# Three edits of a two-block transformer kernel: fewer columns in the last layer's products, expert counts ahead of ranks, down products first in the expert loop

## What is computed

```python
# first block: each token goes to its two best experts of 32 (in one of 4 groups)
y = (jax.nn.silu(hf @ wg) * (hf @ wu)) @ wd        # wg, wu: 1024x256, wd: 256x1024
acc + gate_col[:, None] * y
# second block: 16 meta tokens are put ahead of the 512, and cut off at the end
h = jnp.concatenate([meta, x], axis=1)
for each of two layers:
    h = h + rms_norm(mixer(rms_norm(h, pre), *mix), post)
    h = h + rms_norm(conv_ffn(rms_norm(h, f_pre), w_up, c_w, c_b, w_down), f_post)
return h[:, N_META:]
```

## Time and profile before

| | |
|---|---|
| median of 3 runs | 3109.65 us (3108.88 to 3119.19) |
| the profiled execution, its own time | 3110.36 us |
| its span in the trace | 3108.5 us |
| PE busy | 2854.5 us (92%) |
| DVE, ACT, POOL busy | 1035.6, 620.8, 268.8 us |
| expert loop, first gate-up matmul to last down product read | 619.28 to 940.04 us |
| last layer, out2 to the last product | 2473.4 to 3095.3 us |

### The profile page before, as it was taken

The page is one execution under the profiler, slowest core; times in us unless marked ns, Lnnn a source line. Parts: engine busy times, 40 slices in busy tenths (PEclk is TensorE's granted clock), DMA queues, the critical chain, the costliest instruction groups (busy, mean ns, idle before and its releaser), DMA issues.

```text
span 3108.5 us, 37906 instructions
## 1 busy us (share of the span) xinstructions
PE 2854.5 (92%) x14859; PEld 2136.6 (69%) x14859; DVE 1035.6 (33%) x2148; ACT 620.8 (20%) x1304; POOL 268.8 (9%) x368
## 2 busy tenths in 40 slices
PE   4999887678994999999999999999989899999998
PEld 2554683423332886687888788888877687888787
DVE  6355642311114342604333201113437604333202
ACT  1121220101112453602111001111127402111000
POOL 3121220011220000000000000000006400000000
PEclk7999998689997998999999999999978899999999
DMA  5133102478963111011212122122210011212122
GB/s 226 69 123 122 55 1 122 160 293 356 377 246 126 68 67 56 2 68 55 79 70 73 62 108 108 60 76 68 81 41 2 1 68 58 78 67 81 54 109 81
DMA packets 49449, 312.15 MB, mean 100 GB/s; under 512 B 12192, under 2 KB 14496, under 8 KB 18336
## 3 DMA queue, kind: packets, MB, share of 16 engines
q1 hardware_dynamic: 39520, 290.28, 24.5%
q0 software_dynamic: 9216, 17.85, 1.5%
q10 hardware_dynamic: 576, 2.10, 0.2%
HBM read 351.08 MB, written 16.78 MB: 118 GB/s over the span
## 4 chain that ended last, share of the span: by engine, by line
PE 65%; DVE 2%; ACT 1%; issue 0%; DVEq 0%; POOL 0%; POOLq 0%; ACTq 0%
PE ps L489 35%; PE ps L1001 18%; PE ps L1044 2%; PE ps L966 1%; PE ps L1168 1%; PE ps L984 1%; PE ps L952 1%; PE ps L1140 1%; PE ps L1163 1%; PE ps L991 1%; PE ps L1176 0%; PE ps L1195 0%; PE ps L897 0%; PE ps L1166 0%; PE ps L1118 0%
## 5 line engine op out<-in xcount | busy, mean ns | idle before, releaser
L489 PE MATMUL ps<-u,ring 128*128 128x264 f32 (+1 forms) x5248 | 1253.6, 401 | 27.4 <-DVE u L1675 20.7
L489 PEld LDWEIGHTS ps<-u,ring 128*128 128x128 f32 x5248 | 998.9, 191 | 272.5 <-issue 97.5
L1001 PE MATMUL ps<-work,ring 128*128 128x264 f32 x2432 | 557.6, 389 | 10.8 <-DVE work L1678 8.9
L1001 PEld LDWEIGHTS ps<-work,ring 128*128 128x128 f32 x2432 | 466.4, 192 | 93.5 <-DVE work L1678 9.7
L1675 DVE TENSOR_SCALAR work<-tmp,par 128x528 f32<-128x528 f32 (+2 forms) x136 | 74.9, 551 | 663.6 <-ACT tmp L1578 335.7
L1681 DVE SCALAR_TENSOR_TENSOR work<-tmp,par,work 128x528 f32<-128x528 f32 (+2 forms) x320 | 245.5, 767 | 50.0 <-issue 46.4
L829 PE MATMUL ps<-work,u 128*64 128x512 f32 x640 | 175.4, 615 | 32.3 <-DMA work<-in_experts,rs 30.1
L2285 DVE RECIPROCAL rs<-rs 128x264 f32<-128x264 f32 x8 | 14.4, 1803 | 529.7 <-ACT rs L1520 529.0
L1678 DVE TENSOR_TENSOR work<-work 128x128 f32<-128x128 f32 (+7 forms) x366 | 141.6, 425 | 62.2 <-ACT work L1450 18.4
L1578 ACT ACTIVATE tmp<-ps 128x528 f32<-128x528 f32 x80 | 48.9, 612 | 499.6 <-PE ps L489 499.6
L829 PEld LDWEIGHTS ps<-work,u 128*64 128x64 f32 x640 | 56.7, 142 | 109.5 <-issue 106.6
(11 more groups left out here) (355 smaller groups left out, 2811.5 us busy)
## 6 DMA issues: line engine op xcount, KB each, us to landing
ring<-in_stream SPq DMA_DIRECT2D x169, 1024.0 KB, 4.8
work<-in_experts SPq DMA_DIRECT2D x25, 2048.0 KB, 14.5
work<-in_experts SPq DMA_DIRECT2D x25, 1024.0 KB, 9.3
ring<-in_experts SPq DMA_DIRECT2D x7, 2048.0 KB, 12.6
ring<-in_experts SPq DMA_DIRECT2D x7, 1024.0 KB, 8.7
work<-rows_out SPq DMA_DIRECT2D x4, 1024.0 KB, 8.0
h<-in_x_fm SPq DMA_DIRECT2D x1, 2048.0 KB, 10.7
rows_in<-work ACTq DMA_DIRECT2D x4, 512.0 KB, 2.6
```

The source lines that it names most:

```text
L489: m = pe.matmul(pair(q, half, cnt), ring[:, (n + b // 16) % WSLOTS, b % 16 * P:(b % 16 + 1) * P], x[:, lo:lo + cnt], start=(k == 0), stop= ...
L1001: return pe.matmul(pair(q0 + t, half, HALF), block(t, kk), rhs[kk][:, half * HALF:(half + 1) * HALF], start=(kk == 0), stop=(kk == parts - 1))
```

## The change

Three edits. (1) `product_halves`, `head_tiles` and `out_tile` take a `skip`: the first half of a tile leaves out its first 14 columns (out2, up2) or 16 (down2). (2) PE does the four count matmuls ahead of the ten of the ranks, with a signal of its own; DVE works on counts while PE does ranks, computes the packs by a rounding (three operations on 128x32) in place of seven comparisons, does the softmax of the choices later, and the overflow numbers after `move`; `moves_ready` 1 is now `move` and 2 is `over_id`. (3) In the expert loop, the gate-up product of step s+1 comes after the down product of step s, on ACT and DVE alike; POOL has one wait more ahead of the last `gather_expert`, and waits for `moves_ready` 2 only behind the first row gathers.

```diff
-                    parts = [(0, 0, ncols // 2), (1, ncols // 2, ncols // 2)]
+                    parts = [(0, skip, ncols // 2 - skip), (1, ncols // 2, ncols // 2)]
...
+            for j in range(CHUNKS):
+                m = pe.matmul(ps[:, 7, 128:160], ones, r32[5][:, j, :], start=(j == 0), stop=(j == CHUNKS - 1))
+            m.then_inc(sem("places_done"), 1)
...
             for s in range(len(MSTEPS)):
-                if s + 1 < len(MSTEPS):
-                    gate_up(s + 1)
                 hidden_turned(s)
                 if s + 2 < len(MSTEPS):
                     rows_turned(s + 2)
                 down(s)
+                if s + 1 < len(MSTEPS):
+                    gate_up(s + 1)
...
+                skip = {8: META - CONV_F + 1, 10: META}.get(n, 0)
...
+                skip = META - CONV_F + 1 if n == 10 else 0
...
             for s in range(len(MSTEPS)):
+                if s + 2 < len(MSTEPS):
+                    rows_out_of_psum(s + 2)
                 if s + 1 < len(MSTEPS):
                     gate_silu(s + 1)
-                if s + 2 < len(MSTEPS):
-                    rows_out_of_psum(s + 2)
...
-            ts(e32[1], e32[0], float(MROWS), None, ALU.is_gt)
-            for v in range(2, SEQ // MROWS):
-                dve.drain()
-                stt(e32[1], e32[0], float(MROWS * v), e32[1], ALU.is_gt, add)
+            ts(e32[1], e32[0], -0.5 - MROWS / 2, 1.0 / MROWS, add, mul)
+            dve.drain()
+            ts(e32[1], e32[1], ROUND, None, add)
+            dve.drain()
+            ts(e32[1], e32[1], -ROUND, 0.0, add, hi_)
...
                 hidden_out_of_psum(s)
+                rows_ready(s)
                 if s + 1 < len(MSTEPS):
                     hidden(s + 1)
-                rows_ready(s)
...
             pool.wait_ge(sem("moves_ready"), 1)
-            pool.wait_ge(sem("moves_ready"), 2)
...
+            pool.wait_ge(sem("moves_ready"), 2)
...
                     pool.wait_ge(sem("dn_done"), s + 1)
+                    if MSTEPS[s + 1]:
+                        pool.wait_ge(sem("over_loaded0"), 16 * MSTEPS[:s + 2].count(1))
+                        pool.wait_ge(sem("over_loaded1"), 16 * MSTEPS[:s + 2].count(1))
```

More of the change, by code:

```diff
@@ L473, in unit_wait, with out_tile @@
                 pe.wait_ge(sem(f"unit_loaded{n % WSLOTS}"), 16 * (n // WSLOTS + 1))
-            def out_tile(q, n, b0, rhs, ncols, free, normed=None):
+            def out_tile(q, n, b0, rhs, ncols, free, normed=None, skip=0):
                 pe.wait_ge(sem("tile_read"), free)
@@ L488, in out_tile @@
                             pe.wait_ge(sem("normed"), normed + k + 1)
-                        m = pe.matmul(pair(q, half, cnt), ring[:, (n + b // 16) % WSLOTS, b % 16 * P:(b % 16 + 1) * P],
+                        at0 = 0 if half else skip
+                        m = pe.matmul(ps[:, 2 * (q % 2) + half, at0:at0 + cnt], ring[:, (n + b // 16) % WSLOTS, b % 16 * P:(b % 16 + 1) * P],
                                       x[:, lo:lo + cnt], start=(k == 0), stop=(k == len(rhs) - 1))
@@ L791, in _ @@
             pe.wait_ge(sem("slots_ready"), 1)
+            for j in range(CHUNKS):
+                m = pe.matmul(ps[:, 7, 128:160], ones, r32[5][:, j, :], start=(j == 0), stop=(j == CHUNKS - 1))
+            m.then_inc(sem("places_done"), 1)
             for c in range(CHUNKS):
                 for j in range(c + 1):
[L794 to L797, removed]
+                    m = pe.matmul(ps[:, 1, 32 * c:32 * c + 32], ones if j < c else ccol("strict", 0, P), r32[5][:, j, :],
+                                  start=(j == 0), stop=(j == c))
             m.then_inc(sem("places_done"), 1)
@@ L998, in product_halves @@
                 q0, i0 = Q0[stage], EDGE_SQ(n)
+                skip = {8: META - CONV_F + 1, 10: META}.get(n, 0)
                 def mm(t, half, kk):
-                    return pe.matmul(pair(q0 + t, half, HALF), block(t, kk), rhs[kk][:, half * HALF:(half + 1) * HALF],
-                                     start=(kk == 0), stop=(kk == parts - 1))
+                    lo = 0 if half else skip
+                    return pe.matmul(ps[:, 2 * ((q0 + t) % 2) + half, lo:HALF], block(t, kk),
+                                     rhs[kk][:, half * HALF + lo:(half + 1) * HALF], start=(kk == 0), stop=(kk == parts - 1))
                 for t in range(FULL):
@@ L1035, in product_halves, with head_tiles @@
                 half_sums(i1 + 1, 1, False, True)
-            def head_tiles(stage, n, normed):
+            def head_tiles(stage, n, normed, skip=0):
                 q0, n0, i0 = Q0[stage], U0[stage], EDGE_SQ(n) + 2 + 2 * DT
@@ L1042, in mm @@
                     b = 8 * (t % 2) + kk
-                    out = pair(q0 + t, half, HALF) if t < 2 else ps[:, 4 + half, 0:HALF]
-                    return pe.matmul(out, ring[:, (n0 + t // 2) % WSLOTS, b * P:(b + 1) * P],
-                                     u[:, kk, half * HALF:(half + 1) * HALF], start=(kk == 0), stop=(kk == DT - 1))
+                    bank, lo = (2 * ((q0 + t) % 2) if t < 2 else 4) + half, 0 if half else skip
+                    return pe.matmul(ps[:, bank, lo:HALF], ring[:, (n0 + t // 2) % WSLOTS, b * P:(b + 1) * P],
+                                     u[:, kk, half * HALF + lo:(half + 1) * HALF], start=(kk == 0), stop=(kk == DT - 1))
                 for t in range(3):
@@ L2147, in _ @@
             dve.drain().then_inc(sem("slots_ready"), 1)
-            dve.wait_ge(sem("places_done"), 2)
+            dve.wait_ge(sem("choice_exp"), 1)
+            dve.tensor_reduce(r1[4], r4[1], AX, add)
+            dve.wait_ge(sem("choice_exp"), 2)
+            ts(r1[5], r1[6], 1.0, None, add)
+            dve.drain()
+            tt(r1[4], r1[4], r1[5], mul)
+            dve.drain()
+            dve.reciprocal(r1[7], r1[4])
+            dve.drain()
+            tt(r1[8], r1[7], r1[6], mul)
+            dve.wait_ge(sem("places_done"), 3)
             ts(move_f, ps[:, 7, 0:2 * nst].rearrange("p (t s) -> p t s", t=2), float(NOWHERE), None, add)
@@ L2151, in _ @@
             dve.tensor_copy(move, move_f).then_inc(sem("moves_ready"), 1)
+            tt(ocmp, e32[2].unsqueeze(1).broadcast_to([P, OVER, EXPERTS]),
+               ccol("exp_rank", 0, OVER).unsqueeze(2).broadcast_to([P, OVER, EXPERTS]), add)
+            dve.drain()
+            ts(ocmp, ocmp, float(EXPERTS), None, ALU.is_le)
+            dve.drain()
+            dve.tensor_reduce(orank, ocmp, AX, add)
+            dve.drain()
+            ts(orank, orank, float(P), ccol("row"), mul, add)
+            dve.drain()
+            dve.tensor_copy(over_id, orank).then_inc(sem("moves_ready"), 1)
             def hidden(s):
```

27 lines of the change are left out of this document (6 added, 21 removed).

## The result

The changed kernel took 3079.9 us (median of 4 runs, 3075.7 to 3085.9), the kernel before beside it 3112.6 (4 runs): a ratio of 0.9896, 95% interval 0.9872 to 0.9919, so 32 us less, 25 to 40. The forecast was 3078. The profiled execution took 3083.39, span 3081.6, against 3110.36 and 3108.5.

A forecast was written before the change was run, and what follows sets the result against it. PE's own work (busy 92% of the span), the routing's handovers and waits for overflow weights bound the kernel. From 3109.65 us, columns take 15.6 and routing with loop 15.7, giving 3078; range 3068 to 3092 for 8 in 10.

The forecast's parts named there:

- Columns: In out2, up2 and down2: leaving out 19,072 columns at 0.82 ns each saves 15.6 us, bounds 0 and 15.9.
- lower bound of nothing: In out2, up2 and down2: narrower matmuls save 0 us if a weight load, averaging 190 ns, were the bound.
- Routing: Ahead of the expert loop: `move` is ready 4.9 us earlier and the first gate-up starts 9.6 us earlier, bounds 4.9 and 11.
- the second half: In routing: the first row gather, issued ahead of SP's 3 MB for expert 5, takes 4.3 us instead of 9.0.
- The sign given for it: In routing: the forecast is right if the first row gather comes at 602 to 603 us, first gate-up at 609 to 611.
- Loop: Expert loop, first gate-up to last down copy: shrinks from 320.8 to 314.7 us with the new order.
- steps cost: In the expert loop: PE idles 1.0 us per step for silu and multiply, so 24 steps add 24.0 us.
- slow gate-ups behind them: In the expert loop: slow restarts of gate-ups after weight waits cost 1 us in place of 3.8.
- first two gate-ups: At the start of the expert loop: the new order covers the 2.2 us PE stood between its first two gate-ups.
- Loads late next: In the expert loop: SP's gate-up weights for step 5 land near 679, wanted at 676.4, some 3 us of wait.
- the rival built on it: In the expert loop: idling lowers PE's clock, 1.9 us per step, 46 us over 24 steps, time 3123; chance 5%.
- The loop gives nothing: Loop and routing together give only some 0 to 8 us, so the time is 3086 to 3094; chance 20%.

The follow-up runs named there:

- e1_columns: The kernel before with only the narrower first halves in out2, up2 and down2; 3095.4 us, ratio 0.9953 to the kernel before.
- e12_switch7_again: The changed kernel with the new loop order only in steps 0 to 6, old order after, run again; 3066.5 us, ratio 0.9863 to the kernel before.
- e7_rows_first: The kernel before, with SP holding expert 5's load until the first row gather has landed; 3112.4 us against 3106.2 beside it, routing 28.0 us.
- the switch at 7: The changed kernel with the new loop order in steps 0 to 6 and the old one after; measured twice, 3070.5 and 3066.5 us.
- e4_switch7: The changed kernel with the new loop order only in steps 0 to 6, old order after, on another chip; 3070.5 us, ratio 0.9868 to the kernel before.

## Why the prediction held, point by point

**Columns** (forecast 15.6: out2 2.9, up2 8.1, down2 4.6). Measured 3.3, 7.7 and 6.0 by stage and 14.6 (10 to 19) by the ratio of `e1_columns`. The forecast's 8.1 counts the 704 short records of all up2, the 7.7 only the 656 behind the head. Where the head's clock was as before (`e1_columns`) 0.56 comes on top, 8.2 in all; in the changed kernel's trace the head took 2.5 more instead, so that up2 as a whole gave 5.2. The forecast had no term for the clock there. The size of a column from two stages that differ in shape, 0.82 ns, was right within 2%: 0.833, with 14 columns and with 128. Of the 6.0 of down2 the 352 records give 352 x 13.3 ns = 4.7; the rest is mostly its first two tiles, whose 176 records took 42.47 before, 39.94 in the changed kernel and 40.99 in `e12_switch7_again`, which differs from it nowhere in that stage. The weight load's 190 ns, by which the forecast weighed its lower bound of nothing, was no bound.

**Routing** (forecast 4.9 for `move`, 9.6 for the first gate-up). 5.0 and 10.3. That the second half is the order of two issues was argued from two rows then, and is shown by `e7_rows_first`. The sign given for it, a first row gather at 602 to 603 us, was counted from the start of the routing in the trace before (585.69); this one starts at 582.87, and the gather at 599.38, 16.5 us behind it, as forecast (16.6).

**Loop** (forecast 320.8 to 314.7; measured 316.7). By terms: steps cost 23 x 1.01 = 23.2 (24.0 forecast, for 24 idles: step 0 has none ahead of its transposes); waits went from 30.1 to 6.7 (5); slow gate-ups behind them from 3.8 to 1.5 (1). Mis-sized was the term "first two gate-ups", 2.2: 1.12 of it stands ahead of the first gate-up and so outside the loop, and 0.8 came new ahead of L815. With 0.8 less at the last two steps' copies these terms give 317.2; the 0.5 to the measured value stays open. The waits stood elsewhere than forecast: step 3 waited 4.8 us (0 to 3 forecast), step 6 1.8, step 5 not at all. "Loads late next" named the wrong step: it took SP's queue for what is late, and it was the overflow gather each time. The forecast also took all four waits before for waits for weights; two of them, 2.3 us, were for gathers that carry none.

**Clock in the loop.** It did not fall: 23 idles of 0.94 us, and the gate-ups behind them take 7.04 us as before. In the view of stages the changed kernel has a granted clock of 1.00, the 2.4 GHz level, in this stretch with both the idles and DMA engines full:

```profile
684.00:694.00 10.00, 7.74 (x40) 2.85 (x36) 2.07 (x3) 1.41 (x2) 1.01 (x1) 1.00 1.00 422
```

The rule of the Trainium skill weighed there ("TensorE: Matmul & The Clock Gate", section "A second HAM failure mode: psum-queue depth-cycling"), that frequent small idling costs throughput through the clock, did not show at this size and spacing (0.94 us in each 12.70); the rival built on it would have been 3123.

**Rivals.** "The loop gives nothing" did not come true, but it is near: order alone gives 4.4 us, and without overflow weights it loses 14. That 31.3 was forecast and 31.3 stands in the stages is partly luck: columns 1.3 and routing 0.7 better, the loop 2.0 worse, and the head of up2 left out, with which it is 28.8.

## What to carry to other kernels

Moving a product behind its predecessor's dependent chain cost that chain here in every iteration, and paid only where something late hung on the predecessor: count the idle for all iterations, the lateness for the few that have it, and switch the order where the second ends. Ask whether what is waited for carries anything at all; a gather that moved nothing was still late. When two queues are released by the same event, try issuing the small transfer that the critical engine waits for first. The duration of a load under a matmul did not tell what a shorter matmul would cost; a shape of another size in the same program did.

## What was not expected of the hardware

**The clock's level at a given place differs between executions, and shifts a time by some us.** The routing starts at 582 to 586 us in ten of the fourteen profiles and at 590 to 591 in the four others. Nothing ahead of it is edited, and the switch at 7 is in both groups (590.8 in `e4_switch7`, 583.0 in `e12_switch7_again`).

From the loop's last copy to out2, where nothing is edited either, it is 1531.3 to 1531.4 us in three profiles, 1532.3 to 1533.5 in five and 1537.7 to 1538.3 in six. Here both profiles of the changed kernel have 1538.1 and both of the switch at 7 have 1531.3 to 1531.4. So 6.7 of the 16 us between their medians come from there, and whether that is chance or belongs to the order of the loop is not shown.

In the head of up2, edit 1 narrows half of the records. It took 30.09 us in all five profiles without the edit, and with it 29.53 in three, 30.92 in three and 32.57 in two. The 34 records at its start took 7.80 us without the edit, and 7.41 or 9.09 with it (the chain of work, kernel before, `e1_columns`, changed kernel):

```profile
2602.67 7.80 PE ps L1044 x34
...
2604.93 7.41 PE ps L1047 x34
...
2586.93 9.09 PE ps L1048 x34
```

The view of stages over these records, first the changed kernel, granted clock 0.83:

```profile
2586.00:2596.00 10.00, 9.07 (x35) 7.86 (x36) 9.32 (x20) 0.85 (x2) 0.00 (x0) 0.83 0.15 62
```

then `e1_columns`, with the same records at 1.00:

```profile
2604.00:2613.00 9.00, 8.07 (x38) 7.30 (x39) 8.39 (x18) 0.86 (x3) 0.00 (x0) 1.00 0.16 68
```

In both PE had stood for 1.50 us just before. The lower level at this place was seen only with edit 1 (five profiles of eight, none of five without), so the edit may itself have a part in it; no experiment separates the two, and what decides stays open.

**A gather of 4 KB rows behind 3 MB of plain loads takes 9 us, ahead of them 3.7**, though only 0.9 us lies between the two issues in the one case and 1.6 in the other. PE's wait for the first rows is 10.4 to 10.5 us in the four traces with the plain loads first, and 5.0 to 5.1 in the ten with the gather first.
